# Four modulation buffers outside the Hyena block, and the last four modulation units spread over eight matrix units

## The chip, the cores and the metric

The kernel runs on one core of one Trainium2 chip. The metric is the device time of one execution in microseconds, lower is better. The engines that matter here are PE (TensorE, matrix products), DVE (VectorE), ACT (ScalarE) and SP (SyncE), which only issues DMA transfers.

## What is computed

A diffusion transformer of two layers on 256 latent tokens of width 2048, everything in float32. Layer 0 mixes tokens by attention (8 query heads, 2 key/value heads, with 256 context tokens) and by a gated short convolution, layer 1 by a Hyena long convolution through an FFT. Each layer ends with a squared-ReLU MLP of hidden width 8192. Every block is modulated by vectors that come from the condition c:

```python
def modulate(x, g, shift, scale):
    return rms_norm(x, g) * (1 + scale) + shift

def adaln(cond, w, b):
    return jnp.split(jax.nn.silu(cond) @ w + b, 6, axis=-1)
...
        sh1, sc1, g1, sh2, sc2, g2 = adaln(c[:, None, :], mod_w[l], mod_b[l])
...
            mix_l = jnp.concatenate([latent_attention(q_l, k_l, v_l, k_c, v_c),
                                     short_conv_mixer(pl[..., KV_HI:], ev_conv_w[e])], axis=-1)
            x = x + g1 * (mix_l @ ev_w_out[e])
...
            y = hyena_mixer(modulate(x, norm_mix_g[l], sh1, sc1), od_w_in[o], od_conv_w[o],
                            od_conv_b[o], hyena_filters(n, *fp), od_skip[o])
            x = x + g1 * (y @ od_w_out[o])
...
        x = x + g2 * ffn(modulate(x, norm_ffn_g[l], sh2, sc2), ffn_w1[l], ffn_w2[l])
```

So the weights are of two sorts: those of the large matrix products, with 256 columns of tokens, and `mod_w` (2 x 2048 x 12288), which meets a single vector.

## The kernel before

**Matrix units.** The large products are cut into 93 units. A unit is 2048 input rows by 512 output columns. SP brings its weights in four blocks of 1 MB into `w_raw[kg]`, kg = 0 to 3. ACT copies each block to the reduced float32r format (`w_hi`, two buffers, line 1184), DVE subtracts to get the remainder (`w_lo`, two buffers, line 737), and PE multiplies (line 478): per block 32 matmuls with `w_hi` and 16 with `w_lo`, 192 in a unit, into the four PSUM tiles `acc`. At the end of a unit DVE empties `acc` (line 777 by copy, line 820 into the residual `x`), and only then may PE begin the next (`psum_free`). The order of the units is: keys and values (unit 0), queries (1, 2), then attention, six units of the short convolution (3 to 8), four of the output product (9 to 12), the first MLP (13 to 44), Hyena (45 to 56) and its output (57 to 60), the second MLP (61 to 92).

**Modulation units.** Most of `mod_w` is taken by DVE instead of PE: a modulation unit (`mu`, 40 of them) is 512 columns in eight tiles of 128 x 1024 (512 KB), each loaded into `m_raw[i % 2]` and multiplied with the broadcast condition `wide`, with a sum along the row (line 745, called a tile below). After tile 7 two small operations add the parts and the bias (lines 749 and 751, the pair). `share(n, units, mods)` deals tiles to matrix units: units 0 to 11 take eight each, the first MLP five each, Hyena two or three each. The four modulation units of the last gate (mu 36 to 39) are taken eight tiles a unit in units 61 to 64.

**Who sets the order.** Each engine's program is written out by hand and waits on semaphores. DVE's part of unit u is `body`, where `part` is the unit's tiles in four shares, `fetched` empties `acc` and `post` is what follows (convolution, hidden activation, squares of `x`):

```python
                mod_tiles(part[0])
                lo(u, 2)
...
                mod_tiles(part[1])
                lo(u, 3)
                mod_tiles(part[2])
...
                    lo(u + 1, 0)
                mod_tiles(part[3])
                fetched()
...
                    lo(u + 1, 1)
```

SP issues all weight blocks and tiles from one queue, in program order (`unit`, lines 365 to 376, and `mod_tiles`, lines 354 to 361). It waits for `lo_done` ahead of a weight block (the block of the same kg of the unit before has been split) and for `m_steps` ahead of a tile (DVE has done the tile that had this buffer). With two buffers a tile waits for the one two places ahead of it. `convolution post` below means lines 1033, 1015 and 1022, which follow the second of each three convolution units.

## Time and profile before

| | us |
|---|---|
| median of 3 runs | 2762.68 (2758.9 to 2768.54) |
| the profiled execution's own time | 2763.58 |
| span of its trace | 2761.8 |
| PE busy | 2544.2 |
| DVE busy | 1820.8 |
| ACT busy | 955.9 |
| moved by DMA | 611.40 MB, mean 221 GB/s |

The span runs from the first to the last instruction; some 2 us of the execution's own time lie outside it. A busy share is a mean over stages. The stages here are: startup to 242 us, units 0 to 2 until 360, attention until 449, units 3 to 12 until 741, first MLP until 1518, Hyena and its output until 1961, second MLP to the end. In the waits, "A <- B" means that A stood idle until B had finished.

### The profile page before, as it was taken

What the parts mean: (1) busy time and instruction counts of PE and PEld (TensorE: products, weight loads), DVE (VectorE), ACT (ScalarE), POOL (GpSimd) and SP (SyncE); (2) the same over time, 40 slices, a digit from 0 to 9 for tenths busy, and PEclk for the clock granted to TensorE, in tenths of its full rate; (3) what the DMA queues carried; (4) which work ended last, traced back from release to release, by engine and by line L of the source; (5) the groups of instructions that cost most, each with busy time, mean ns of one, the idle gap of its engine ahead of it and who ended that gap; (6) DMA issues with size and microseconds to landing.
All of it is one profiled execution on the core that took longest, in us unless ns stands there. A gap on an engine that the chain in (4) does not pass through costs nothing.

```text
span 2761.8 us, 49389 instructions
## 1 busy us (share of the span) xinstructions
PE 2544.2 (92%) x19040; PEld 2355.4 (85%) x19040; DVE 1820.8 (66%) x2645; ACT 955.9 (35%) x958; POOL 0.2 (0%) x4
## 2 busy tenths in 40 slices
PE   6797978887899999999999899999879999999997
PEld 1224957887799999999999899999779999999997
DVE  1305665777787688787787778785776555555555
ACT  1314223222344333333343322233423333333333
POOL 0000000000000000000000000000000000000000
PEclk9798989998899999999999899999989999999998
DMA  7463824777578788788788556664586555555552
GB/s 269 140 197 131 279 87 149 273 271 280 199 273 293 261 292 300 274 297 298 266 296 297 185 197 216 234 222 157 167 283 215 181 182 182 182 182 181 182 182 101
DMA packets 266384, 611.40 MB, mean 221 GB/s; under 512 B 12245, under 2 KB 12373, under 8 KB 266014
## 3 DMA queue, kind: packets, MB, share of 16 engines
q1 hardware_dynamic: 260766, 598.93, 63.2%
q10 hardware_dynamic: 5504, 10.83, 1.1%
q8 instruction: 86, 1.41, 0.2%
q14 instruction: 28, 0.23, 0.0%
HBM read 603.43 MB, written 6.29 MB: 221 GB/s over the span
## 4 chain that ended last, share of the span: by engine, by line
PE 80%; DMA 8%; DVE 6%; issue 4%; ACT 2%; DVEq 0%; SPq 0%; ACTq 0%
PE acc L478 68%; DMA m_raw<-mod_rest 7%; PE acc L539 4%; PE aux L527 1%; PE aux L683 1%; PE aux L703 1%; DVE m_raw L745 1%; PE aux L475 1%; ACT w_hi L1184 1%; PE aux L516 1%; DVE summed L853 1%; PE acc L645 1%; DVE w_lo L737 1%; PE aux L519 0%; DVE x L820 0%
## 5 line engine op out<-in xcount | busy, mean ns | idle before, releaser
L737 DVE TENSOR_TENSOR w_lo<-w_raw,w_hi 128x2048 fp32r<-128x2048 f32 x372 | 851.1, 2289 | 459.9 <-ACT w_hi L1184 456.2
L1184 ACT ACTIVATE w_hi<-w_raw 128x2048 fp32r<-128x2048 f32 x372 | 712.1, 1915 | 1271.3 <-PE acc L478 1251.4
L478 PE MATMUL acc<-act_a,w_hi 128*128 128x256 f32 x6784 | 897.7, 290 | 70.4 <-DVE summed L777 30.8
L478 PEld LDWEIGHTS acc<-act_a,w_hi 128*128 128x128 f32 x6784 | 868.7, 198 | 76.9 <-issue 32.9
L478 PE MATMUL acc<-act_b,w_hi 128*128 128x256 f32 x5120 | 651.2, 286 | 28.6 <-DVE summed L777 14.8
L478 PEld LDWEIGHTS acc<-act_b,w_hi 128*128 128x128 f32 x5120 | 635.0, 195 | 31.2 <-DVE summed L777 15.4
L745 DVE SCALAR_TENSOR_TENSOR m_raw<-m_raw,wide 128x1024 f32<-128x1024 f32 x320 | 387.7, 1221 | 99.9 <-DMA m_raw<-mod_rest 99.2
L478 PE MATMUL acc<-act_a,w_lo 128*128 128x256 f32 x3392 | 448.8, 283 | 0.0
L478 PEld LDWEIGHTS acc<-act_a,w_lo 128*128 128x128 f32 x3392 | 426.7, 192 | 0.0
L478 PE MATMUL acc<-act_b,w_lo 128*128 128x256 f32 x2560 | 333.3, 283 | 0.0
L478 PEld LDWEIGHTS acc<-act_b,w_lo 128*128 128x128 f32 x2560 | 318.7, 192 | 0.0
L1184 ACT ACTIVATE act_b<-worked 128x256 f32 (+1 forms) x152 | 54.3, 420 | 203.3 <-DVE worked L798 122.5
L539 PE MATMUL acc<-w_raw,silu 128*2 128x512 f32 x256 | 115.1, 609 | 3.8 <-ACT late L1184 3.8
L890 DVE SCALAR_TENSOR_TENSOR summed<-worked,aux 128x512 f32<-128x512 f32 x16 | 10.3, 684 | 145.8 <-ACT worked L1184 145.8
L820 DVE SCALAR_TENSOR_TENSOR x<-acc,mv,x 128x256 f32 (+1 forms) x160 | 71.8, 481 | 49.6 <-PE acc L478 49.1
L539 PEld LDWEIGHTS acc<-w_raw,silu 128*2 128x2 f32 x256 | 21.5, 86 | 96.0 <-issue 91.4
L777 DVE COPY summed<-acc 128x256 f32<-128x256 f32 x192 | 75.4, 422 | 31.8 <-PE acc L478 27.2
L811 DVE TENSOR_TENSOR sq_sum<-sq_sum,worked 128x256 f32<-128x256 f32 x192 | 81.4, 424 | 21.2 <-ACT worked L1184 13.3
L1184 ACT ACTIVATE worked<-x 128x256 f32 (+1 forms) x176 | 62.1, 406 | 27.8 <-DVE x L820 23.9
L787 DVE TENSOR_TENSOR act_b<-worked,act_b 128x256 f32 (+1 forms) x152 | 54.4, 422 | 0.2 <-issue 0.2
L527 PE MATMUL aux<-scr,wide 128*128 128x512 f32 x64 | 38.1, 761 | 15.3 <-DVE scr L894 15.3
L527 PEld LDWEIGHTS aux<-scr,wide 128*128 128x128 f32 x64 | 15.5, 249 | 38.6 <-DVE scr L894 19.4
(129 smaller groups left out, 911.5 us busy)
## 6 DMA issues: line engine op xcount, KB each, us to landing
w_raw<-ffn_w SPq DMA_DIRECT2D x256, 1024.0 KB, 6.5
m_raw<-mod_rest SPq DMA_DIRECT2D x320, 512.0 KB, 5.2
w_raw<-od_w_in SPq DMA_DIRECT2D x48, 1024.0 KB, 7.0
w_raw<-ev_w_in SPq DMA_DIRECT2D x36, 1024.0 KB, 7.8
w_raw<-mod_first SPq DMA_DIRECT2D x32, 1024.0 KB, 5.2
w_raw<-ev_w_out SPq DMA_DIRECT2D x16, 1024.0 KB, 7.5
w_raw<-od_w_out SPq DMA_DIRECT2D x16, 1024.0 KB, 5.1
scr<-k_freq ACTq DMA_DIRECT2D x8, 512.0 KB, 5.8
```

The lines of the kernel that those rows point to most:

```text
L475: mm = pe.matmul(aux[ft][:, 0:n], w, act_b[:, k, a:a + n], start=start, stop=stop)
L478: mm = pe.matmul(acc[ft][:, 0:n], w, rhs[:, k, a:a + n], start=start, stop=stop)
L516: pe.matmul(aux[i][:, :], fh[0:FHID, i, tt * P:tt * P + P], m_raw[0:FHID, 0, i * 512:i * 512 + 512], start=True, stop=True)
L527: mm = pe.matmul(aux[r][:, :], fwd_first[:, tt, r * P:r * P + P], (f_sum if r < 2 else f_dif)[:, tt, :], start=(tt == 0), stop=(tt == 1))
L539: mm = pe.matmul(acc[tt][0:2, :], silu[:, 0, k:k + 17:16], w_raw[:, kg, kc * 512:kc * 512 + 512], start=(k == 0), stop=(k == 15))
L737: TT(w_lo[:, kg % 2, :], w_raw[:, kg, :], w_hi[:, kg % 2, :].bitcast(F32), ALU.subtract)\
L745: STT(out=raw, in0=raw, scalar=1.0, in1=wide[:, i % 2 * 1024:i % 2 * 1024 + 1024], op0=ALU.mult, op1=ALU.mult, accum_out=m_part[:, i:i + 1 ...
L777: dve.tensor_copy(dst, acc[ft][:, 0:T]).then_inc(psum_free, 1)
L787: TT(act_b[:, c, T:2 * T], worked[:, ft, :], act_b[:, c, 0:T].bitcast(F32), ALU.subtract)\
L811: TT(sq_sum[:, :], sq_sum[:, :], worked[:, slot, :], ALU.add).then_inc(sq_steps, 1)
L820: STT(out=xc, in0=acc[ft][:, 0:T], scalar=mv[:, ds(m * 4 + (gate + ft), 1)], in1=xc, op0=ALU.mult, op1=ALU.add).then_inc(psum_free, 1)
L1184: return act.activation(out_, in_, func, **kw)
```

## The change

- **Buffers.** Outside Hyena a tile goes to one of four buffers: the two halves of `m_raw` and two pieces of the scratch area `scr`. Up to unit 2 these are `scr[4096:5120]` and `scr[6144:7168]` (`EARLY`), afterwards `scr[2048:4096]` (`WIDE`), which attention uses for keys and values. In Hyena both sides of `scr` are in use, and the two buffers stay (`NARROW`). The wait is for the tile four places ahead (`i - 3`), in Hyena two (`i - 1`). There are four semaphores `m_landed`.
- **SP's order.** In unit u SP now issues, behind its four weight blocks in turn, tiles 4 and 5 of unit u-1, tiles 6 and 7 of unit u-1, tiles 0 and 1 of unit u, tiles 2 and 3 of unit u. This holds in Hyena too. Behind the fourth block of unit 3 SP waits for the end of attention (`o_full`), since tiles 2 and 3 go where keys and values were. The convolution units are written out instead of looped.
- **Second MLP.** The last four modulation units are dealt four tiles a unit to units 61 to 68, with the helper of the first MLP (`mlp_mods`, formerly `mlp0`).
- PE's and ACT's programs are the same.

```diff
+        def m_slots(early):
+
+            spare = (4096, 6144) if early else (2048, 3072)
+            return [m_raw[:, 0, :], m_raw[:, 1, :]] + [scr[:, a:a + 1024] for a in spare]
+
+        EARLY, WIDE = m_slots(True), m_slots(False)
+        NARROW = [m_raw[:, i % 2, :] for i in range(4)]
-        m_landed = [sem(f"m_landed{i}") for i in range(2)]
+        m_landed = [sem(f"m_landed{i}") for i in range(4)]
-            def mod_tiles(tiles):
+            def mod_tiles(tiles, slots):
 
                 for mu, i in tiles:
-                    if not (isinstance(mu, int) and mu == 0 and i < 2):
+                    if isinstance(mu, int) and mu == 0 and i < 4:
+                        if i == 2:
+                            sp.wait_ge(kf_full, 16)
+                            sp.wait_ge(row_turned, START)
+                    elif isinstance(mu, int) and mu == MU_F1 and i < 4:
+                        sp.wait_ge(m_steps, MU_F1 * 8)
+                    elif slots is NARROW:
                         sp.wait_ge(m_steps, mu * 8 + (i - 1))
-                    sp.dma_start(m_raw[:, i % 2, :], mod_rest[ds(mu * 512 + i // 2 * P, P), i % 2 * 1024:i % 2 * 1024 + 1024])\
-                        .then_inc(m_landed[i % 2], 16)
-
-            def unit(u, w, row, col, own=(), before=(), first=False):
+                    else:
+                        sp.wait_ge(m_steps, mu * 8 + (i - 3))
+                    sp.dma_start(slots[i % 4], mod_rest[ds(mu * 512 + i // 2 * P, P), i % 2 * 1024:i % 2 * 1024 + 1024])\
+                        .then_inc(m_landed[i % 4], 16)
+
+            def unit(u, w, row, col, own=(), before=(), first=False, slots=WIDE, old=None):
...
-                    mod_tiles(before[2 * kg + 2:2 * kg + 4] if kg < 3 else own[0:2])
+                    if kg < 2:
+                        mod_tiles(before[2 * kg + 4:2 * kg + 6], old or slots)
+                    else:
+                        mod_tiles(own[2 * kg - 4:2 * kg - 2], slots)
-            unit(U_KV, ev_w_in, 0, ATTN_W, mods(0), first=True)
-            unit(U_Q, ev_w_in, 0, 0, mods(1), mods(0))
-            unit(U_Q + 1, ev_w_in, 0, 512, mods(2), mods(1))
-            with sp.Fori(0, 2) as j:
-                for n, col in enumerate((2 * CONV_W, 0, CONV_W)):
-                    unit(j * 3 + (U_CONV + n), ev_w_in, 0, j * 512 + (KV_HI + col), mods(j * 3 + (3 + n)),
-                         mods(j * 3 + (2 + n)))
...
+            def conv_unit(j, n, old=None):
+                unit(j * 3 + (U_CONV + n), ev_w_in, 0, j * 512 + (KV_HI + (2 * CONV_W, 0, CONV_W)[n]),
+                     mods(j * 3 + (3 + n)), mods(j * 3 + (2 + n)), old=old)
+
+            for kg in range(4):
+                sp.wait_ge(lo_done, (U_CONV - 1) * 4 + (kg + 1))
+                sp.dma_start(w_raw[:, kg, :].rearrange("p (c n) -> p c n", c=4),
+                             ev_w_in[kg * 512:kg * 512 + 512, KV_HI + 2 * CONV_W:KV_HI + 2 * CONV_W + 512]
+                             .rearrange("(c p) n -> p c n", p=P)).then_inc(landed[kg], 16)
+                if kg < 2:
+                    mod_tiles(mods(2)[2 * kg + 4:2 * kg + 6], EARLY)
+                else:
+                    if kg == 3:
+                        sp.wait_ge(o_full, N_Q)
+                    mod_tiles(mods(3)[2 * kg - 4:2 * kg - 2], WIDE)
+            conv_unit(0, 1)
+            conv_unit(0, 2)
+            for n in range(3):
+                conv_unit(1, n)
             with sp.Fori(0, 3) as m:
                 unit(m + U_EVOUT, ev_w_out, 0, m * 512, mods(m + 9), mods(m + 8))
             unit(U_EVOUT + 3, ev_w_out, 0, 3 * 512, (), mods(11))
...
-            def mlp0(q, u, mu):
+            def mlp_mods(q, u, w_row, w2_row, mu, count, before):
+
 
                 for n in range(8):
-                    w, row, col = (ffn_w1, 0, q * 2048) if n < 4 else (ffn_w2, q * 2048, 0)
-                    if n:
-                        before = mods(mu, share(n - 1, 8, 5))
-                    else:
-                        before = () if isinstance(q, int) else mods(mu - 5, share(7, 8, 5))
-                    unit(u + n, w, row, col + n % 4 * 512, mods(mu, share(n, 8, 5)), before)
-
-            def mlp1(q, u, mod=None):
-
-                unit(u, ffn_w1, D_MODEL, q * 2048, mod(0) if mod else ())
-                with sp.Fori(1, 4) as m:
-                    unit(u + m, ffn_w1, D_MODEL, q * 2048 + m * 512, mod(m) if mod else (), mod(m - 1) if mod else ())
-                unit(u + 4, ffn_w2, q * 2048 + D_FF, 0, (), mod(3) if mod else ())
-                with sp.Fori(1, 4) as m:
-                    unit(u + m + 4, ffn_w2, q * 2048 + D_FF, m * 512)
-
-            mlp0(0, U_F0, MU_F0)
+                    w, row, col = (ffn_w1, w_row, q * 2048) if n < 4 else (ffn_w2, q * 2048 + w2_row, 0)
+                    unit(u + n, w, row, col + n % 4 * 512, mods(mu, share(n, 8, count)),
+                         mods(mu, share(n - 1, 8, count)) if n else before)
+
+            mlp_mods(0, U_F0, 0, 0, MU_F0, 5, ())
...
+            def hyena(j, before, old=NARROW):
                 for n, col in enumerate((1, 2, 0)):
                     unit(j * 3 + (U_D - 3 + n), od_w_in, 0, j * 512 + (col * D_MODEL - 512),
                          mods(j + (MU_D - 1), share(n, 3, 1)),
-                         mods(j + (MU_D - 1), share(n - 1, 3, 1)) if n else before)
-
-            hyena(1, mods(MU_D - 5, share(7, 8, 5)))
+                         mods(j + (MU_D - 1), share(n - 1, 3, 1)) if n else before, slots=NARROW, old=None if n else old)
...
+            hyena(1, mods(MU_D - 5, share(7, 8, 5)), WIDE)
+            sp.wait_ge(b_made, 96)
+            mlp_mods(0, U_F1, D_MODEL, D_FF, MU_F1, 4, ())
             with sp.Fori(1, 4) as q:
-                mlp1(q, q * 8 + U_F1)
+                u = q * 8 + U_F1
+                with sp.Fori(0, 4) as m:
+                    unit(u + m, ffn_w1, D_MODEL, q * 2048 + m * 512)
+                with sp.Fori(0, 4) as m:
+                    unit(u + m + 4, ffn_w2, q * 2048 + D_FF, m * 512)
...
-            def mod_tiles(tiles):
+            def mod_tiles(tiles, slots):
 
                 for mu, i in tiles:
-                    dve.wait_ge(m_landed[i % 2], mu * 64 + 16 * (i // 2 + 1))
-                    raw = m_raw[:, i % 2, :]
+                    dve.wait_ge(m_landed[i % 4], mu * 32 + 16 * (i // 4 + 1))
+                    raw = slots[i % 4]
                     STT(out=raw, in0=raw, scalar=1.0, in1=wide[:, i % 2 * 1024:i % 2 * 1024 + 1024], op0=ALU.mult,
                         op1=ALU.mult, accum_out=m_part[:, i:i + 1]).then_inc(m_steps, 1)
...
-            body(U_KV, keys_values, mod=0)
+            body(U_KV, keys_values, mod=0, slots=EARLY)
             with own.loop(2, 0) as m:
-                body(m + U_Q, lambda: queries(m), mod=m + 1)
...
-                    body(u + m, lambda: sums(u + m), lambda: hidden(u + m, m, q * 16 + f0 + m * 4), mod(m) if mod else None)
+                    body(u + m, lambda: sums(u + m), lambda: hidden(u + m, m, q * 16 + f0 + m * 4))
                 clear_squares(step)
-                if mod:
-                    dve.wait_ge(mv_ready, MU_F1 + 4)
```

Two places of SP's program on which terms of the prediction rest. The first is between the last query unit and the second convolution unit. SP's program before, from the last weight block of unit 2 (`L373`) on; the loop over the convolution units begins with the branch, and its rows that are not DMA are register work and waits:

```order
L373 DMA w_raw<-ev_w_in 128x4x512 [waits lo_done]
L360 DMA m_raw<-mod_rest 128x1024 [waits m_steps] x2
L401 UNCONDITIONAL_BRANCH
L401 ISA
L373 ISA [waits lo_done]
L373 DMA w_raw<-ev_w_in 128x4x512
L359 ISA
L360 ISA [waits m_steps]
L360 DMA m_raw<-mod_rest 128x1024
```

SP's program of the change, from the third weight block of unit 3 on:

```order
L427 DMA w_raw<-ev_w_in 128x4x512 [waits lo_done]
L376 DMA m_raw<-mod_rest 128x1024 [waits m_steps] x2
L427 DMA w_raw<-ev_w_in 128x4x512 [waits lo_done]
L376 DMA scr<-mod_rest 128x1024 [waits m_steps,o_full]
L376 DMA scr<-mod_rest 128x1024 [waits m_steps]
L389 DMA w_raw<-ev_w_in 128x4x512 [waits lo_done]
L376 DMA m_raw<-mod_rest 128x1024 [waits m_steps] x2
```

Two tiles still follow each weight block, now by turns in `m_raw` and `scr`, and tiles 2 and 3 of unit 3 have the wait for `o_full` ahead of them, and behind them stands the first weight block of unit 4. The second place is the first three Hyena units, 45 to 47. SP's program before, from the third block of unit 45 on:

```order
L373 DMA w_raw<-od_w_in 128x4x512 [waits lo_done] x2
L360 DMA m_raw<-mod_rest 128x1024 [waits m_steps] x2
L373 DMA w_raw<-od_w_in 128x4x512 [waits lo_done] x4
L360 DMA m_raw<-mod_rest 128x1024 [waits m_steps] x2
L373 DMA w_raw<-od_w_in 128x4x512 [waits lo_done]
L360 DMA m_raw<-mod_rest 128x1024 [waits m_steps]
L373 DMA w_raw<-od_w_in 128x4x512 [waits lo_done] x3
```

and SP's program of the change, from the second block of unit 45 on:

```order
L389 DMA w_raw<-od_w_in 128x4x512 [waits lo_done] x2
L376 DMA m_raw<-mod_rest 128x1024 [waits m_steps] x2
L389 DMA w_raw<-od_w_in 128x4x512 [waits lo_done] x4
L376 DMA m_raw<-mod_rest 128x1024 [waits m_steps] x2
L389 DMA w_raw<-od_w_in 128x4x512 [waits lo_done]
L376 DMA m_raw<-mod_rest 128x1024 [waits m_steps]
L389 DMA w_raw<-od_w_in 128x4x512 [waits lo_done] x3
```

The rows look alike, but they stand for other blocks. Before, the four loads in one row are the blocks of unit 46, the tile pair behind them its tiles 2 and 3, and the single load is the first block of unit 47, behind which comes tile 4. Now the four are the last block of unit 45 and the first three of unit 46, the single load is the last block of unit 46, and tile 4 stands behind it, ahead of the first block of unit 47.

## Rows read from the trace of the kernel before

**Rows 1.** Page: busy time of each engine, share of the span, instructions.
```profile
PE 2544.2 (92%) x19040; PEld 2355.4 (85%) x19040; DVE 1820.8 (66%) x2645; ACT 955.9 (35%) x958; POOL 0.2 (0%) x4
```

**Rows 2.** Windows: start:end length, busy us (x count) per engine, clock, DMA share, GB/s.
```profile
303.65:359.67 56.02, 47.99 (x387) 47.59 (x385) 42.49 (x58) 15.33 (x8) 0.00 (x0) 0.96 0.81 279
448.84:627.82 178.98, 148.83 (x1153) 147.61 (x1153) 131.83 (x193) 47.41 (x28) 0.00 (x0) 0.91 0.81 278
627.82:716.22 88.40, 75.01 (x576) 74.40 (x576) 67.72 (x96) 27.61 (x24) 0.00 (x0) 0.90 0.80 284
1976.97:2097.16 120.19, 98.84 (x760) 98.03 (x758) 92.05 (x141) 38.52 (x35) 0.00 (x0) 0.90 0.79 268
766.30:789.30 23.00, 23.00 (x194) 23.00 (x193) 20.27 (x28) 9.06 (x9) 0.00 (x0) 1.00 0.89 311
473.95:501.04 27.09, 24.78 (x193) 24.58 (x193) 20.34 (x27) 7.66 (x4) 0.00 (x0) 0.94 0.92 320
593.97:627.82 33.85, 24.80 (x193) 24.60 (x193) 25.82 (x43) 7.67 (x4) 0.00 (x0) 0.86 0.72 247
1420.00:1430.00 10.00, 10.00 (x85) 10.00 (x85) 9.99 (x19) 4.11 (x6) 0.00 (x0) 1.00 1.03 391
```

**Rows 3.** Waits 448 to 742: who waited for whom, us in total, times, longest.
```profile
DVE m_raw L745 <- DMA m_raw<-mod_rest: 52.6, 46, 3.0
...
PE acc L478 <- DVE summed L777: 23.2, 4, 9.0
...
PE acc L478 <- DVE x L820: 13.4, 3, 5.8
```

**Rows 4.** Timeline 464 to 513: start, us, engine, line, op, [idle before].
```profile
464.49 1.92 ACT L1184 ACTIVATE w_hi<-w_raw 128x2048 fp32r<-128x2048 f32 x1 [3.85 <-PE acc L478]
...
466.53 2.29 DVE L737 TENSOR_TENSOR w_lo<-w_raw,w_hi 128x2048 fp32r<-128x2048 f32 x1
...
498.87 1.22 DVE L745 SCALAR_TENSOR_TENSOR m_raw<-m_raw,wide 128x1024 f32<-128x1024 f32 x1 [1.11 <-DMA m_raw<-mod_rest]
...
500.56 1.41 DVE L777 COPY summed<-acc 128x256 f32<-128x256 f32 x4
...
501.04 5.59 PE L478 MATMUL acc<-act_a,w_hi 128*128 128x256 f32 x32 [2.31 <-DVE summed L777]
...
501.89 2.28 DVE L737 TENSOR_TENSOR w_lo<-w_raw,w_hi 128x2048 fp32r<-128x2048 f32 x1
504.09 1.43 DVE L1033 TENSOR_TENSOR summed<-summed,scr 128x256 f32<-128x256 f32 x4
...
509.92 1.22 DVE L745 SCALAR_TENSOR_TENSOR m_raw<-m_raw,wide 128x1024 f32<-128x1024 f32 x1
...
512.21 2.29 DVE L737 TENSOR_TENSOR w_lo<-w_raw,w_hi 128x2048 fp32r<-128x2048 f32 x1
```

**Rows 5.** Timeline 345 to 362, the end of the second query unit.
```profile
358.19 1.42 DVE L777 COPY scr<-acc 128x256 f32 x4
...
359.67 1.97 PE L593 MATMUL acc<-tab,scr 128*128 128x128 f32 x8 [3.69 <-DVE scr L777]
```

**Rows 6.** Chain that ended last, piece of the last 28 units.
```profile
2097.16 646.43 PE acc L478 x5364
```

**Rows 7.** Timeline of PE 1998 to 2125, first units of the second MLP.
```profile
2007.24 5.60 PE L478 MATMUL acc<-act_a,w_hi 128*128 128x256 f32 x32 [7.07 <-DVE summed L777]
...
2103.57 2.08 PE L478 MATMUL acc<-act_b,w_lo 128*128 128x256 f32 x16
```

**Rows 8.** Waits of PE 752 to 1530, the first MLP.
```profile
PE acc L478 <- issue: 12.6, 3, 4.6
...
PE acc L478 <- DVE summed L777: 1.0, 1, 1.0
```

**Rows 9.** Page, DMA issues: count, KB each, median us to landing.
```profile
m_raw<-mod_rest SPq DMA_DIRECT2D x320, 512.0 KB, 5.2
w_raw<-od_w_in SPq DMA_DIRECT2D x48, 1024.0 KB, 7.0
```

More of the change, by code:

```diff
@@ L397, in _ @@
             sp.wait_ge(h_full, 8)
-            unit(U_KV, ev_w_in, 0, ATTN_W, mods(0), first=True)
-            unit(U_Q, ev_w_in, 0, 0, mods(1), mods(0))
-            unit(U_Q + 1, ev_w_in, 0, 512, mods(2), mods(1))
-            with sp.Fori(0, 2) as j:
-                for n, col in enumerate((2 * CONV_W, 0, CONV_W)):
-                    unit(j * 3 + (U_CONV + n), ev_w_in, 0, j * 512 + (KV_HI + col), mods(j * 3 + (3 + n)),
-                         mods(j * 3 + (2 + n)))
+            unit(U_KV, ev_w_in, 0, ATTN_W, mods(0), first=True, slots=EARLY)
+            unit(U_Q, ev_w_in, 0, 0, mods(1), mods(0), slots=EARLY)
+            unit(U_Q + 1, ev_w_in, 0, 512, mods(2), mods(1), slots=EARLY)
+            def conv_unit(j, n, old=None):
[16 more added lines that the diff above has]
+                conv_unit(1, n)
             with sp.Fori(0, 3) as m:
@@ L752, in mod_tiles, with body @@
                            vec[:, ds(mu * 4 + (VEC["mod_b"][0] + 32), 4)], ALU.add).then_inc(mv_ready, 1)
-            def body(u, fetched, post=None, mod=None, tiles=EIGHT, mid=None, last=False):
+            def body(u, fetched, post=None, mod=None, tiles=EIGHT, mid=None, last=False, slots=WIDE):
                 tiles = [] if mod is None else [(mod + m, i) for m, i in tiles]
                 part = [tiles[len(tiles) * i // 4:len(tiles) * (i + 1) // 4] for i in range(4)]
-                mod_tiles(part[0])
+                mod_tiles(part[0], slots)
                 lo(u, 2)
@@ L762, in body @@
                     mid()
-                mod_tiles(part[1])
+                mod_tiles(part[1], slots)
                 lo(u, 3)
-                mod_tiles(part[2])
+                mod_tiles(part[2], slots)
                 if not last:
                     lo(u + 1, 0)
-                mod_tiles(part[3])
+                mod_tiles(part[3], slots)
                 fetched()
@@ L1066, in mlp0, with mlp @@
                         clear_squares(step)
-                    v, tiles = u + n, share(n, 8, 5)
+                    v, tiles = u + n, share(n, 8, count)
+                    gate = 80 + 96 * layer
                     if n >= 4:
-                        body(v, lambda: residual(v, n - 4, 80, 9 + n),
+                        body(v, lambda: residual(v, n - 4, gate, first_gate + n - 3),
                              lambda: x_squares(xu + (n - 4), step + (n * 4 - 15)), mu, tiles)
                     else:
-                        body(v, lambda: sums(v), lambda: hidden(v, n, q * 16 + (16 + n * 4)), mu, tiles)
-            def mlp(q, u, layer, f0, xu, step, mod=None, final=False):
+                        body(v, lambda: sums(v), lambda: hidden(v, n, q * 16 + f0 + n * 4), mu, tiles)
+            def mlp(q, u, layer, f0, xu, step, final=False):
                 with own.loop(4, 0) as m:
-                    body(u + m, lambda: sums(u + m), lambda: hidden(u + m, m, q * 16 + f0 + m * 4), mod(m) if mod else None)
+                    body(u + m, lambda: sums(u + m), lambda: hidden(u + m, m, q * 16 + f0 + m * 4))
                 clear_squares(step)
-                if mod:
-                    dve.wait_ge(mv_ready, MU_F1 + 4)
                 gate = 80 + 96 * layer
@@ L1151, in hyena @@
                     body(j * 3 + (U_D + n), lambda: sums(j * 3 + (U_D + n)), lambda: post(j),
-                         j + MU_D, share(n, 3, 1),
+                         j + MU_D, share(n, 3, 1), slots=NARROW,
                          mid=None if n or first else (lambda: convolved(j - 1)))
```

13 lines of the change are left out of this document (6 added, 7 removed).

## The prediction

> **What bounds the kernel now.** I read the busy shares first. PE is busy for 2544.2 us, 92% [rows 1], so the kernel is bound by PE plus the places where PE stands. Next I asked what one matrix unit takes when nothing is in its way. The last piece of the chain of waits runs over the last 28 units (65 to 92) in 646.43 us [rows 6]; less 2.6 us for a slow start (below) that is 23.0 us a unit. The stretch 766.30 to 789.30, in the first MLP with five tiles a unit, shows the same: PE busy for all 23.00 us [rows 2]. So 23.0 us is the floor.
>
> Then the windows of the stages with eight tiles a unit [rows 2]. Units 1 and 2 take 56.0 us (floor 46.0), the six convolution units 179.0 us (138.0), units 9 to 11 88.4 us (69.0), and units 61 to 64 120.2 us (92.0). The granted clock there is 0.90 to 0.96 instead of 1.00. What ends PE's waits is DVE emptying `acc`: 23.2 us in four waits and 13.4 us in three [rows 3]. What delays DVE is its own wait for tiles, 52.6 us in 46 waits [rows 3]. The chain reads: a tile lands late, DVE reaches the evacuation late, PE starts the next unit late. Each late start costs twice. At 501.04 PE had been idle for 2.31 us, and its first 32 matmuls took 5.59 us [rows 4] instead of the 4.0 us of others; the granted clock over that unit is 0.94 [rows 2], so for a moment it was the lower of the two levels, 1.2 instead of 2.4 GHz. I take 1.6 us for this slow group behind a wait of about 2 us or more, and up to 2.6 us behind longer ones.
>
> **The change part by part.** It adds no arithmetic: 320 tiles, the same pairs, the same PE program. It gives a tile four places of lead instead of two. At the floor a place is 23.0 / 8 = 2.9 us; four of them less the 1.15 us of the tile itself leave 10.3 us from the issue to the need, against 4.6 us with two. The median landing time is 5.2 us [rows 9]: longer than 4.6, shorter than 10.3. So I remove DVE's waits for tiles and ask what is late next.
>
> DVE's own work in a unit with eight tiles [rows 4]: a tile 1.15 us (509.92 to 512.21 is two), so 9.2; the pair 0.54 (498.87 to 500.56, less a tile), so 0.6; four `w_lo` at 2.2 (501.89 to 504.09), so 8.8; the evacuation 1.33 (500.56 to 501.89). Sum 19.9 us. The convolution post adds 5.8 (504.09 to 509.92) in every third unit, the others less: about 3 for the gate and 2 for the squares, estimates from the four-instruction groups of 1.4 us.
>
> *An ordinary unit.* Let PE start at S. ACT's copy for the next unit's first block comes 15.6 us later (464.49, where S is 448.9), DVE's `w_lo` at S + 17.6 (466.53). Add 2.2, two tiles 2.3 and the pair 0.6: the evacuation starts at S + 22.7, and PE follows 0.48 behind it (500.56 to 501.04), at S + 23.2. That is 0.2 over the floor, with too short a wait for a slow group (estimate).
>
> *Units 1 and 2.* Unit 2 starts at 326.7 instead of 331.2, without its slow group, and its evacuation begins at 326.7 + 22.8 = 349.5. The transposes of attention follow 1.48 us behind such a start (358.19 to 359.67 [rows 5]), at 351.0 instead of 359.67: **8.6 us** gained. Attention itself keeps its length. At its end tiles 2 and 3 of unit 3 now wait for `o_full`, and the first block of unit 4 is queued behind them. Tiles 2 and 3 are needed some 9 us after it, the block some 15: with 5.2 and 7 us to land, that costs nothing.
>
> *Convolution and output, units 3 to 11.* Unit 3: 23.2. Unit 4: 23.2. Behind unit 4 DVE has the post, and its cycle from one evacuation to the next is 19.9 + 5.8 = 25.7 us, which puts unit 6 at 49.0 us behind the start of unit 4 instead of 46.2. Unit 5 therefore lasts 26.0 with 2.8 us of waiting at its end, and unit 6 has the slow group, 24.8. Units 7, 8 and 9 repeat 4, 5 and 6; units 10 and 11 take 23.2. Sum: 23.2 + 23.2 + 26.0 + 24.8 + 23.2 + 26.0 + 24.8 + 23.2 + 23.2 = 217.6 us, against 267.4 (448.84 to 716.22 [rows 2]): 49.8 gained, and 1.6 for the slow group of unit 12: **51.4 us**.
>
> *First MLP.* It has one wait for DVE of 1.0 us [rows 8], 1.2 with its edges, behind a late tile: **1.2 us**. The three waits marked issue, 12.6 us together [rows 8], fall where PE's own loop turns back; PE's program is the same, and I leave them.
>
> *Second MLP.* PE stood for 7.1 us ahead of unit 62, which began at 2007.24 [rows 7]; units 62 to 64 took 89.9 us (2007.24 to 2097.16 [rows 6, 7]) for 69.1; unit 65 had a slow group of 6.4 instead of 3.8 (2097.16 to 2103.57). Excess 7.1 + 20.8 + 2.6 = 30.5. With four tiles in eight units, fewer than the five under which the first MLP runs at its floor [rows 2], all of it goes: **30.5 us**.
>
> *Hyena.* Still two buffers, but the single tile now stands ahead of the first weight block of the next unit. That block is issued about 10 us into a unit and needed at 15.6 to 17; it takes 7.0 us to land [rows 9]. PE itself needs the result only at 23.0, so I cost it at nothing. Bounds: a gain of nothing, a loss of 2 us in each of eight units, 16 us.
>
> *The transfers.* Eleven units (1 to 11) move 92.3 MB (8.39 MB each). By the sums above they last 47.4 + 217.6 = 265.0 us, which asks for 348 GB/s, and 363 GB/s in those near the floor. The trace before bounds this from both sides: 320 GB/s at a DMA share of 0.92 in the best unit with eight tiles, 391 GB/s over the best 10 us [rows 2]. 320 at 0.92 means about 348 at a full share, 311 at 0.89 about 349. I take 349, the nearest kind of row, which makes 24.0 us for each of the five units that are not slowed by the post (1, 2, 9 to 11): 0.8 to 1.0 each, **5 us** lost. At 391 it is 0, at 320 it is 23.
>
> A page of the Trainium skill speaks against part of this: "DMA: Bandwidth & Descriptors", section Specifications, gives about 358 GB/s as the limit of HBM for one core, by which, as an estimate, a unit would take 23.4 us and the loss would be 2 us instead of 5; that changes no chance, since it stays inside my forecast's spread. The 391 GB/s of [rows 2] are above it, if only for 10 us.
>
> Sum: 8.6 + 51.4 + 1.2 + 30.5 - 5 = 86.7 us off 2763.6, the profiled execution's own time: 2676.9. The median of the runs is 0.9 below that execution, so 2676.
>
> **Rivals.**
> - *DMA bound.* At the best unit's 320 GB/s the eleven units take 288.4 instead of 270 us: 2695. For it: 320 was reached while tiles were late, so much was queued. Against it: the share there was 0.92, not 1. Chance 0.15.
> - *Late by a little.* If a tile or block still comes 1 us late in each of eleven units, every start has its wait and its slow group: 11 x 2.6 = 29 us, less the 5 already counted: 2700. For it: landing is 5.2 us in the median, not at most. Chance 0.08.
> - *Better.* The transfers cost nothing and the post's 10 us are partly hidden, or the issue waits shrink: 2663. Chance 0.09.
> - *It does not do what it says.* One SP queue in program order: tiles are held behind weight blocks that wait, and the lead stays at two in the stages with eight tiles. Then only 30.5 and 1.2 us remain: 2731, taken from 2762.7. Against it: a block's wait (`lo_done` of the unit before) is nearly always fulfilled when its turn comes. Chance 0.04.
> - *Slower.* The mix of tiles and blocks, more of them in flight, moves at a lower rate. At the 247 GB/s of unit 8 (593.97 to 627.82), the lowest window [rows 2], the eleven units take 374 us instead of 323.4, a loss of 50 against 32 gained elsewhere: 2781. It decides below 92.3 MB / 355 us = 260 GB/s. Unit 8 shows 247 GB/s, but at a DMA share of 0.72, so it was short of requests and not of rate, and the windows of whole stages lie at 278 and more [rows 2]. Chance 0.02.
> - *No change* from causes that cancel: 0.02.
>
> **The numbers.** My forecast has 0.60. Predicted 2676. The forecast's own spread is 2668 to 2686; down to the better case and up over both DMA cases, 2660 to 2704, leaves out some 0.1. A measurement of this kernel tells 0.3%, 8 us, from no change. Faster 0.96, same 0.02, slower 0.02.
>
> **What would show it.** Right: DVE's waits for tiles between the end of startup and the second MLP nearly gone; unit lengths of 23 to 24 us, with 26 for units 5 and 8; units 61 to 68 at 23.0; DMA near 350 GB/s in units 1, 2 and 9 to 11; attention and Hyena as long as before; three issue waits left. Wrong: `w_hi` on ACT waiting for `w_raw` from DMA, in Hyena above all, or unit lengths of 26 us with the DMA share near 1.

## The result and the profile after

The changed kernel takes 2667.14 us in the median of 4 runs (2661.42 to 2669.68), beside 2760.79 before (2757.38 to 2768.54): ratio 0.9655, 95% interval 0.9632 to 0.9677. The forecast was 2676, with a range from 2660 to 2704. The two profiled executions have spans of 2761.8 and 2667.9 us, 93.9 apart, and the stages are compared on these.

The page of the changed kernel: busy time, granted clock and rate in 40 slices, the chain that ended last, the groups of the tiles (they answer to [rows 1]) and the DMA issues (as [rows 9]).

```profile
PE 2517.2 (94%) x19040; PEld 2327.9 (87%) x19040; DVE 1812.4 (68%) x2645; ACT 955.7 (36%) x958; POOL 0.2 (0%) x4
...
PEclk9788989999899999999998999999899999999998
...
GB/s 278 144 170 188 251 97 159 340 335 334 220 291 295 292 294 299 281 297 291 288 298 215 208 195 189 228 231 154 189 274 273 202 175 186 185 177 189 177 185 94
...
PE 86%; DVE 7%; DMA 2%; issue 2%; ACT 2%; DVEq 0%; SPq 0%; ACTq 0%
...
L774 DVE SCALAR_TENSOR_TENSOR m_raw<-m_raw,wide 128x1024 f32<-128x1024 f32 x176 | 211.9, 1217 | 0.4
L774 DVE SCALAR_TENSOR_TENSOR scr<-scr,wide 128x1024 f32<-128x1024 f32 x144 | 173.2, 1219 | 0.0
...
m_raw<-mod_rest SPq DMA_DIRECT2D x176, 512.0 KB, 5.6
scr<-mod_rest SPq DMA_DIRECT2D x144, 512.0 KB, 6.4
w_raw<-od_w_in SPq DMA_DIRECT2D x48, 1024.0 KB, 8.5
```

DVE stood 0.4 us ahead of all 320 tiles together; before, 52.6 us between 448 and 742 alone [rows 3]. A tile takes longer to land than before (5.6 and 6.4 us, not 5.2 [rows 9]) and is still in time. A block of `od_w_in` takes 8.5 instead of 7.0 [rows 9], which matters below.

Windows of the changed kernel (start:end length, busy us of each engine, clock, DMA share, GB/s): unit 2, units 4 to 8, one of them, unit 11, and units 62 to 65 (by the marks of the table below), to be held against [rows 2]:

```profile
309.00:332.00 23.00, 22.89 (x191) 22.68 (x190) 20.59 (x29) 7.26 (x5) 0.00 (x0) 1.00 0.91 337
443.40:563.50 120.10, 117.71 (x962) 116.93 (x962) 106.37 (x154) 39.72 (x24) 0.00 (x0) 0.99 0.96 358
467.00:490.00 23.00, 23.00 (x192) 22.87 (x192) 19.81 (x28) 7.45 (x5) 0.00 (x0) 1.00 1.01 373
614.00:637.60 23.60, 23.35 (x194) 23.15 (x194) 21.85 (x32) 9.29 (x9) 0.00 (x0) 1.00 0.96 345
1918.30:2009.90 91.60, 91.60 (x766) 91.60 (x765) 72.77 (x101) 36.41 (x33) 0.00 (x0) 1.00 0.78 264
```

PE is busy for 118 of 120 us in units 4 to 8; before, it stood for 30 of the 179 us of units 3 to 8 [rows 2]. The DMA engines carry 373 GB/s over a whole unit.

What each stage gave, measured from ACT's copy of the third block of one unit to that of the next (so "unit 6" ends when PE has been in unit 6 for 4 us, or for 5.6 us where it began slowly, and holds PE's wait ahead of it); the forecast has the price of the transfers dealt out as it was counted:

| stage | forecast | measured |
|---|---|---|
| startup and unit 0 | 0 | -0.8 |
| units 1 to 3, attention between them | 8.6 - 2.0 | 10.4 |
| units 4 to 12 | 51.4 - 3.0 | 51.1 |
| units 13 to 20 | 1.2 | 1.3 |
| the first MLP behind them, all of it in units 21, 29 and 37 | 0 | 12.9 |
| Hyena and its output, units 45 to 60 | 0 | -10.5 |
| second MLP | 30.5 | 30.2 |
| sum | 86.7 | 94.6 |

(0.7 us of it is lost behind the last unit, which leaves the 93.9 of the spans.) The mark of unit 0 lies anywhere from 270.7 to 273.9 us in the twelve traces of this case, whatever the edit, so 3 us between two whole times say nothing of an edit. The two large rows forecast as zero nearly cancel. The experiments are about these two, and about which part of the change does what.

**Where Hyena lost.** Waits of the changed kernel, 1470 to 1910:

```profile
ACT w_hi L1213 <- DMA w_raw<-od_w_in: 51.9, 11, 8.0
...
PE acc L507 <- DVE summed L806: 5.9, 4, 2.0
```

Neither wait exists before in this stage. Its timeline in PE's unit 52, where the first block of unit 53 is fetched (start, us, engine, line, op, idle before):

```profile
1664.27 0.08 DVE L774 DVE_READ_ACCUMULATOR m_raw<-m_raw,wide 128x1 f32 x1
1664.53 0.33 SPq L376 DMA_DIRECT2D m_raw<-mod_rest  x1
...
1665.16 1.67 SPq L389 DMA_DIRECT2D w_raw<-od_w_in  x3
...
1673.08 1.92 ACT L1213 ACTIVATE w_hi<-w_raw 128x2048 fp32r<-128x2048 f32 x1 [7.64 <-DMA w_raw<-od_w_in]
...
1677.33 1.22 DVE L774 SCALAR_TENSOR_TENSOR m_raw<-m_raw,wide 128x1024 f32<-128x1024 f32 x1
...
1678.47 1.42 DVE L806 COPY summed<-acc 128x256 f32<-128x256 f32 x4
...
1678.95 2.31 PE L507 MATMUL acc<-act_a,w_hi 128*128 128x256 f32 x14 [2.03 <-DVE summed L806]
```

Unit 52 began on PE at 1653.72. With two buffers the tile's request waits for the tile two places ahead, done at 1664.27. Three weight blocks stand behind it in SP's queue and are requested together, at 1665.16 and after. The first is there at 1673.08, 19.4 us into the unit; ACT could have copied it at 15.6. DVE is then late at the evacuation, PE stands for 2.03 us, and a slow group follows: from mark to mark (unit 53 of the table's measure) this took 26.8 us instead of 23.0.

**Where the first MLP gained.** Units 21, 29 and 37 hold the places where PE's own loop over the quarters turns back. They took 30.0, 29.7 and 30.0 us before and take 25.1, 26.7 and 25.0 now; the `issue` waits of [rows 8] are gone and these stand there (waits of PE in the changed kernel, 700 to 1470):

```profile
PE acc L507 <- DVE x L849: 5.5, 3, 2.0
```

Before: the first turn, timeline of PE and DMA queues (share of 16 engines) from 943 to 945.

```profile
940.39 2.08 PE L478 MATMUL acc<-act_b,w_lo 128*128 128x256 f32 x16
946.61 1.65 PE L478 MATMUL acc<-act_a,w_hi 128*128 128x256 f32 x6 [4.14 <-issue]
...
q1 hardware_dynamic: 301, 0.76, 102.1%
q8 instruction: 1, 0.02, 3.2%
```

After: the same turn, DMA queues from 879 to 881.

```profile
878.35 2.08 PE L507 MATMUL acc<-act_b,w_lo 128*128 128x256 f32 x16
882.26 1.94 PE L507 MATMUL acc<-act_a,w_hi 128*128 128x256 f32 x14 [1.83 <-DVE x L849]
...
q1 hardware_dynamic: 122, 0.42, 73.7%
q8 instruction: 1, 0.02, 3.9%
```

### The profile page after: what moved, and what is told of

The parts are those of the page before. It is cut to its first block, busy times and chain, and to the rows that moved or that the text cites. A ratio compares the mean times of both kernels' runs of the same rounds, so it can differ in the third digit from the quotient of the medians.

```text
span 2667.9 us, 48783 instructions
## 1 busy us (share of the span) xinstructions
PE 2517.2 (94%) x19040; PEld 2327.9 (87%) x19040; DVE 1812.4 (68%) x2645; ACT 955.7 (36%) x958; POOL 0.2 (0%) x4
## 4 chain that ended last, share of the span: by engine, by line
PE 86%; DVE 7%; DMA 2%; issue 2%; ACT 2%; DVEq 0%; SPq 0%; ACTq 0%
PE acc L507 74%; PE acc L568 4%; PE aux L556 1%; DMA w_raw<-od_w_in 1%; DVE w_lo L766 1%; PE aux L712 1%; PE aux L504 1%; ACT w_hi L1213 1%; PE aux L732 1%; PE aux L545 1%; DMA scr<-k_freq 1%; DVE m_raw L774 1%; PE acc L674 1%; DVE x L849 0%; PE aux L548 0%
## 5 line engine op out<-in xcount | busy, mean ns | idle before, releaser
L507 PE MATMUL acc<-act_a,w_hi 128*128 128x256 f32 x6784 | 879.1, 286 | 29.6 <-DVE act_a L887 14.5
L507 PEld LDWEIGHTS acc<-act_a,w_hi 128*128 128x128 f32 x6784 | 850.0, 194 | 36.1 <-issue 19.7
L507 PE MATMUL acc<-act_b,w_hi 128*128 128x256 f32 x5120 | 643.1, 284 | 3.5 <-DVE summed L806 2.4
L507 PEld LDWEIGHTS acc<-act_b,w_hi 128*128 128x128 f32 x5120 | 627.2, 192 | 5.7 <-DVE x L849 2.6
L774 DVE SCALAR_TENSOR_TENSOR m_raw<-m_raw,wide 128x1024 f32<-128x1024 f32 x176 | 211.9, 1217 | 0.4
L774 DVE SCALAR_TENSOR_TENSOR scr<-scr,wide 128x1024 f32<-128x1024 f32 x144 | 173.2, 1219 | 0.0
L849 DVE SCALAR_TENSOR_TENSOR x<-acc,mv,x 128x256 f32<-128x256 f32 (+1 forms) x160 | 71.5, 481 | 43.9 <-PE acc L507 43.9
L840 DVE TENSOR_TENSOR sq_sum<-sq_sum,worked 128x256 f32<-128x256 f32 x192 | 81.4, 424 | 22.5 <-ACT worked L1213 13.9
L816 DVE TENSOR_TENSOR act_b<-worked,act_b 128x256 fp32r<-128x256 f32 (+1 forms) x152 | 54.2, 420 | 0.2 <-issue 0.2
```

Of the source, the lines that this page charges most:

```text
L507: mm = pe.matmul(acc[ft][:, 0:n], w, rhs[:, k, a:a + n], start=start, stop=stop)
L774: STT(out=raw, in0=raw, scalar=1.0, in1=wide[:, i % 2 * 1024:i % 2 * 1024 + 1024], op0=ALU.mult, op1=ALU.mult, accum_out=m_part[:, i:i + 1 ...
L816: TT(act_b[:, c, T:2 * T], worked[:, ft, :], act_b[:, c, 0:T].bitcast(F32), ALU.subtract)\
L840: TT(sq_sum[:, :], sq_sum[:, :], worked[:, slot, :], ALU.add).then_inc(sq_steps, 1)
L849: STT(out=xc, in0=acc[ft][:, 0:T], scalar=mv[:, ds(m * 4 + (gate + ft), 1)], in1=xc, op0=ALU.mult, op1=ALU.add).then_inc(psum_free, 1)
```

## The experiments

Each is one edit to the changed kernel unless said otherwise. The edits are shown in part, `...` marks what is left out, and ratios are to the kernel before on the same chip, which had a median of 2761.15 (experiments 1 to 4), 2764.47 (5 to 8) and 2761.98 (9 and 10).

### 1. Hyena with SP's old order

```diff
+                    if slots is NARROW and old is not WIDE:
+                        mod_tiles(before[2 * kg + 2:2 * kg + 4] if kg < 3 else own[0:2], slots)
...
```

> The changed kernel, but in Hyena SP issues in the order of the kernel before: the single tile behind the first weight block of the next unit, the tile pair behind the last block of its own unit. Theory A (a weight block queued behind a tile that waits, then three blocks at once, comes too late for ACT): the 11 us that units 46 to 57 lost against before come back, 2656, and ACT's waits for od_w_in from DMA (51.9 us in the changed kernel) fall under 10. Rival B (Hyena lost by another phase of the k_freq loads or of DVE, not by the order of SP): 2667 as the changed kernel.

Measured: 2655.93 us (2653.07 to 2659.26), ratio 0.9626 (0.9591 to 0.9661). Units 47, 50, 53 and 56 are back at 23.0 us, and ACT waits for no block of `od_w_in` any more. The loss in Hyena comes from the order of SP's queue, not from the bus: the same bytes move with the same two buffers.

### 2. First MLP with two buffers and the old order

```diff
+                    elif order == "old":
+                        mod_tiles(before[2 * kg + 2:2 * kg + 4] if kg < 3 else own[0:2], slots)
...
-            mlp_mods(0, U_F0, 0, 0, MU_F0, 5, ())
+            mlp_mods(0, U_F0, 0, 0, MU_F0, 5, (), slots=NARROW, order="old")
...
```

> The changed kernel, but the first MLP has two buffers and SP's order of before; everything else of the change stays. It tells where the 12.9 us at the three turns of PE's loop came from (units 21, 29 and 37 took 30.0, 29.7, 30.0 us from second to third ACT copy before, 25.1, 26.7, 25.0 in the changed kernel). Theory A (PE fetches its instructions over the same DMA engines, and the fetch at a turn stands behind whatever SP had just issued; with the old order more is queued there): the three turns take 30 us again, the issue waits of PE are back at 4 us each, the late tile of unit 17 is back, 2681. Rival B (the turns have nothing to do with the tiles' order; an effect of alignment elsewhere): 2667 to 2669.

Measured: 2679.81 us (2678.02 to 2681.77), ratio 0.9709 (0.9674 to 0.9743). The edit also changes where SP issues the last tiles of the first MLP, in the first Hyena unit; Hyena as a whole loses 8.9 us here. The turn units are at 30.7, 29.8 and 30.0. The waits of PE there:

```profile
PE acc L511 <- issue: 14.0, 3, 5.0
```

So the length of PE's loop turns depends on how SP issues. Buffers or order? The next one tells.

### 3. Four buffers, but the old order everywhere

```diff
-                    if kg < 2:
-                        mod_tiles(before[2 * kg + 4:2 * kg + 6], old or slots)
-                    else:
-                        mod_tiles(own[2 * kg - 4:2 * kg - 2], slots)
...
+                    mod_tiles(before[2 * kg + 2:2 * kg + 4] if kg < 3 else own[0:2], old if kg < 3 else slots)
...
```

The wait for the end of attention moves with the tiles, behind the first block of unit 4.

> Four buffers outside Hyena and the spread of the last four modulation units, but everywhere SP's order of the kernel before. Theory A (what counts is four places of lead; SP's order only costs in Hyena): units 3 to 12 as in the changed kernel within 5 us, Hyena as before, 2655 to 2662 by where the loop turns of the first MLP land. Rival B (the new order is needed, since with the old one the second pair of tiles stands behind the first weight block of the next unit): tile waits on DVE return in units 1 to 12, over 20 us, 2690 or more.

Measured: 2669.9 us (2667.95 to 2672.04), ratio 0.9677 (0.9643 to 0.9711). Units 3 to 12 and the second MLP are as in the changed kernel (units 6 and 9 27.6 and 26.6, unit 10 22.8), Hyena is as before, but the turn units take 29.1, 29.4 and 29.7 with the wait back:

```profile
PE acc L508 <- issue: 13.1, 3, 4.6
```

The expectation was missed because it took the shorter turns for a gift of the four buffers. They come from the new order. So the buffers (with the spread) give the gains in units 1 to 12 and the second MLP, and the new order gives some 11 us at the turns and takes as much in Hyena: the two kernels' intervals overlap.

### 4. The new order with two buffers everywhere

```diff
-        EARLY, WIDE = m_slots(True), m_slots(False)
-        NARROW = [m_raw[:, i % 2, :] for i in range(4)]
+        EARLY = WIDE = NARROW = [m_raw[:, i % 2, :] for i in range(4)]
...
```

> SP's new order and the spread, but two buffers everywhere. Theory A (lead is what counts; at two places it is 4.6 us against 5.2 to land): the waits of DVE for tiles return in units 1 to 12 in full, and weight blocks are in addition held behind tiles that wait; 60 us of the gain are lost and some more, 2725 to 2760. Rival B (the order alone brings most of it): under 2690.

Measured: 2828.08 us (2820.28 to 2829.22), ratio 1.0239 (1.02 to 1.0278): slower than before by some 67 us, and outside what was expected. The spread is in this kernel too and is worth 30 us by itself (experiment 5), so by the two ratios the new order costs some 98 us where there are two buffers. The whole trace's waits:

```profile
ACT w_hi L1208 <- DMA w_raw<-ffn_w: 367.4, 73, 8.4
...
DVE m_raw L769 <- DMA m_raw<-mod_rest: 62.6, 51, 3.0
```

and the timeline in the first MLP, where five tiles a unit ran at the floor before:

```profile
817.16 4.02 SPq L371 DMA_DIRECT2D m_raw<-mod_rest  x2
...
821.22 0.43 SPq L384 DMA_DIRECT2D w_raw<-ffn_w  x1
...
827.57 1.91 ACT L1208 ACTIVATE w_hi<-w_raw 128x2048 fp32r<-128x2048 f32 x1 [6.55 <-DMA w_raw<-ffn_w]
```

SP stands at the second of two tiles until a buffer is free, and the weight block behind it goes out late. The first MLP alone loses 75 us, with nearly every unit at 24 to 28. This is what happened in Hyena, at two or three tiles a unit, made large. The new order asks for tiles earlier, and with no free buffer to take them that only holds up the blocks.

### 5. The kernel before, with only the last modulation units spread

```diff
-            mlp1(0, U_F1, lambda m: mods(m + MU_F1))
+            mlp0(0, U_F1, MU_F1, D_MODEL, D_FF, 4)
...
```

> The kernel before (two buffers, old order) with the spread of the last four modulation units over units 61 to 68 alone. Theory A (four tiles a unit leave two buffers enough lead, as five do in the first MLP): all 30.5 us of the second MLP are gained and nothing else changes, 2730. Rival B (it needs four buffers as well): DVE's tile waits stay in part, 2740 or more.

Measured: 2730.43 us (2727.51 to 2733.54), ratio 0.9885 (0.9866 to 0.9904). Units 62 to 65 take 22.5 to 23.0 us. This is also the time that the rival "it does not do what it says" named.

### 6. The changed kernel without the spread

```diff
+    if (units, mods) == (8, 4):
+        return [(n, i) for i in range(8)] if n < 4 else []
```

> The changed kernel without the spread: eight tiles in each of units 61 to 64, with four buffers. Theory A (DVE needs 19.9 us and 3 us of post in such a unit, so four buffers alone nearly suffice): 23.2 to 23.8 us a unit, 2668 to 2671. Rival B (eight tiles a unit need the spread, since transfers or DVE are too slow there): units of 25 us or more, 2676 or more.

Measured: 2664.53 us (2663.79 to 2667.3), ratio 0.9646 (0.9629 to 0.9663), no slower than with it. Window over units 62 to 65, eight tiles each:

```profile
1912.40:2004.20 91.80, 91.80 (x767) 91.80 (x766) 89.53 (x137) 36.40 (x32) 0.00 (x0) 1.00 0.94 344
```

PE has no gap and DVE is busy for 89.5 of 91.8 us. So either part alone gives the 30 us of the second MLP, and with four buffers the spread is idle.

### 7. Evacuation ahead of the last two tiles in units 5 and 8

On top of experiment 1.

```diff
+                if soon:
+                    fetched()
                 mod_tiles(part[3], slots)
-                fetched()
+                if not soon:
+                    fetched()
...
```

> Hyena in the old order of SP (as in the run before, 2656) and in units 5 and 8 DVE empties the accumulators ahead of the last two tiles of the unit instead of behind them. Theory A (units 5 and 8 last 27.2 us from copy to copy because DVE, with the convolution post, reaches the evacuation 3 us late): PE starts units 6 and 9 without a wait and without its slow group, 4 us each, 2648. Rival B (DVE's work in the three units is the bound, so what is saved at unit 6 is lost at its end): 2655.

Measured: 2654.21 us (2653.19 to 2657.31), ratio 0.9609 (0.9592 to 0.9627). From the mark of unit 3 to that of unit 12 its trace takes 214.3 us, that of experiment 1 takes 217.7. PE does start units 6 and 9 without a wait, but it then stands ahead of units 7 and 10. PE in both, first experiment 1, then this one:

```profile
509.55 5.58 PE L511 MATMUL acc<-act_a,w_hi 128*128 128x256 f32 x32 [2.38 <-DVE summed L810]
583.16 5.42 PE L511 MATMUL acc<-act_b,w_hi 128*128 128x256 f32 x32 [2.39 <-DVE summed L810]
...
531.52 4.10 PE L511 MATMUL acc<-act_a,w_hi 128*128 128x256 f32 x32 [2.26 <-DVE scr L813]
603.62 4.09 PE L511 MATMUL acc<-act_b,w_hi 128*128 128x256 f32 x32 [2.55 <-DVE x L856]
```

The waits are as long as in experiment 1, 4.8 us for the two: what is saved ahead of unit 6 is lost ahead of unit 7, as rival B says. Of the 3.4 us, 2.8 are the first groups behind the waits, 5.58 and 5.42 us there, 4.10 and 4.09 here. The granted clock over the two groups here is 1.00. In the whole time, 2654.21, this can't be told from experiment 1 or from rival B's 2655: one of its turn units took 26.7 instead of 24.8 us, again by a slow first group.

### 8. PE's loop over the quarters of the first MLP written out

```diff
-            with pe.Fori(0, 4) as q:
+            for q in range(4):
```

> The changed kernel with PE's loop over the four quarters of the first MLP written out, so that PE has no jump back at units 21, 29 and 37. Theory A (the rest of the waits there, 25.1, 26.7 and 25.0 us for 23.0, is the fetch of instructions behind a jump): these units take 23.0, 7.8 us gained, 2659. Rival B (the waits come from DVE or from the transfers of weights at that place): 2667. It could also cost, if PE then waits for instructions all along.

Measured: 2657.25 us (2651.88 to 2658.75), ratio 0.961 (0.9591 to 0.9629). The turn units take 23.5, 23.4 and 23.4. So what remained of the turns in the changed kernel was the loop's own.

### 9. More data in front of the instructions

```diff
+                    if spare and kg == 3:
+                        for a in (4096, 6144 - 1024):
+                            sp.dma_start(scr[:, a:a + 1024], mod_rest[0:P, 0:1024]).then_inc(spare_landed, 16)
+                        sp.dma_start(scr[:, 6144:7168], mod_rest[0:P, 0:1024]).then_inc(spare_landed, 16)
+                        sp.dma_start(scr[:, 0:1024], mod_rest[0:P, 0:1024]).then_inc(spare_landed, 16)
...
+                    if n == 3 and not isinstance(q, int):
+                        sp.wait_ge(spare_landed, q * 64)
```

> The changed kernel, with four more transfers of 512 KB each (modulation weights, read into a buffer that nobody uses) requested behind the last weight block of the first unit of quarters 1 to 3 of the first MLP; the computation is unchanged. Theory A (at a loop turn TensorE's instructions are fetched over the same DMA engines and stand behind whatever data is queued there): each of the three turn units 21, 29 and 37 grows from about 25 to 29 or 30 us, issue waits of TensorE come back in the list of waits, the time is about 2680. Theory B (the length of a turn has nothing to do with queued data): the turn units stay at 25 to 27 us, no issue waits, 2665 to 2671.

Measured: 2677.36 us (2673.65 to 2679.42), ratio 0.9696 (0.9675 to 0.9717). The turn units are at 29.4, 28.9 and 29.3 us, the others as they were. The waits of PE in the first MLP, PE at the first turn, and the DMA queues from 881 to 882:

```profile
PE acc L515 <- issue: 13.4, 3, 4.7
...
876.95 2.08 PE L515 MATMUL acc<-act_b,w_lo 128*128 128x256 f32 x16
883.75 3.50 PE L515 MATMUL acc<-act_a,w_hi 128*128 128x256 f32 x15 [4.72 <-issue]
...
q1 hardware_dynamic: 108, 0.38, 102.2%
q8 instruction: 1, 0.02, 6.1%
```

PE finished at 879.03. The instruction packet starts at 881.0 and takes 0.97 us (6.1% of 16 engines for 1 us), so PE starts 1.8 us behind its end, as in the two traces above. PE's program and the tiles are those of the changed kernel; only queued data was added, and 10.8 of the 12.9 us came back.

The same is seen at every turn. Ten of the twelve traces keep PE's loop (all but experiments 8 and 10), which makes 30 turns. By the DMA records PE starts 1.75 to 1.88 us behind the end of such a packet in all 30. In the 18 turns of the kernel before and of experiments 2, 3, 4, 5 and 9 the packet begins 0.8 to 2.2 us after PE has run dry, and the data queue's share in the 2 us ahead of it was 0.98 or more. In the 12 of the changed kernel and of experiments 1, 6 and 7 it begins 0.8 to 1.2 us before PE is done, at a share of 0.50 to 0.96.

### 10. Experiments 1, 7 and 8 together

> Three edits to the changed kernel at once: the Hyena block goes back to the old order of its requests with two modulation buffers, units 5 and 8 put their evacuation before their last two tiles, and TensorE's loop over the quarters of the first MLP is written out. Theory A (the three act at different places and so add up): 2655.9 from the Hyena edit alone, less 7 to 10 us for the loop turns, less 2 to 4 us for the evacuations, about 2646. Theory B (the gains overlap, because work that comes earlier only meets the next late transfer): 2652 to 2656, no better than the Hyena edit with the evacuations.

Measured: 2647.81 us (2647.33 to 2649.67), ratio 0.9589 (0.9571 to 0.9606), the fastest of all. The page and the window over units 4 to 8:

```profile
span 2647.4 us, 48550 instructions
...
PE 91%; DVE 5%; issue 2%; ACT 1%; DMA 1%; DVEq 0%; ACTq 0%; SPq 0%
```

```profile
443.40:563.50 120.10, 117.82 (x977) 117.20 (x977) 108.06 (x159) 41.50 (x25) 0.00 (x0) 1.00 0.97 362
```

It is 19 us below the changed kernel: by the trace 10.8 in Hyena (units 45 to 60) and 6.6 in the turn units (76.8 down to 70.2). Of the 20.5 us between the two spans that leaves 3.1, and the trace is ahead by as much at unit 12, behind the two evacuations that were moved.

## Why the prediction was right

**What bounds the kernel** held: late tiles, late evacuation, late PE. With the lateness gone DVE's waits for tiles are gone and ordinary units take 23.2 to 23.5 us.

**Units 3 to 11** held nearly to the term: 51.4 less 3 forecast, 51.1 measured. The working of the post (of `convolution post`) is visible as it was put. Timeline of the changed kernel at the end of unit 5:

```profile
510.96 1.41 DVE L806 COPY summed<-acc 128x256 f32<-128x256 f32 x4
...
511.44 5.58 PE L507 MATMUL acc<-act_a,w_hi 128*128 128x256 f32 x32 [2.39 <-DVE summed L806]
```

PE waits 2.39 us (2.8 forecast; the 26.0 of the sum should have been 25.7 by its own cycle of DVE) and then has the slow group of 5.58 instead of 4.0. Unit 6 by the table's marks is 27.2 us; 2.8 and 1.6 over 23.2 would be 27.6.

**The slow group** was priced rightly at 1.6 us, but in part by a wrong row: the clock of 0.94 is that of the unit ahead of 501.04, which had a slow group of its own at 473.95. The group at 501.04 itself shows 0.69:

```profile
501.04:503.50 2.46, 2.46 (x15) 2.46 (x16) 2.46 (x4) 0.00 (x0) 0.00 (x0) 0.69 0.89 288
```

That it comes behind "a wait of about 2 us or more" came true in units 6 and 9 and is no rule (experiment 7, and the last section).

**Units 1 and 2**: the products of attention begin at 352.05 us, against 351.0 forecast and 359.67 before, so 7.6 of the 8.6 came; the 2 us taken off for transfers did not. "Attention itself keeps its length" did not hold: up to unit 3 it takes 87.3 us instead of 89.2. The 1.9 us lie in its first products, 11.5 instead of 13.6 us up to PE's first long wait, at a granted clock of 0.67 instead of 0.50, behind a wait of 1.08 instead of 3.69 us.

**The transfers** were mis-sized: 5 us forecast. The step that failed is the one from "320 GB/s at a share of 0.92" to "348 at a full share". A share did not stand for the same rate in the two kernels: the changed one shows 337 at 0.91, 358 at 0.96 and 373 at 1.01, which is some 370 for a full share, where the rows before gave 349. Units 10 to 12 still took 0.3 us each over the 23.2 of the forecast, so about 1 of the 5 us may be real. The rival "DMA bound" is out: its 320 GB/s are passed in every window above with eight tiles a unit. The Trainium skill's figure of 358 GB/s for a core ("DMA: Bandwidth & Descriptors", Specifications) is passed too, over a whole unit; the section Measured of the same page gives 425 for a single core in transfers of 16 MB, and the highest window shown here, 404 over 2.6 us, stays below it.

**First MLP, issue waits**: the step "PE's program is the same, and I leave them" failed. The program was the same, but the time in which its instructions arrive was not: 12.9 us gained. The forecast looked for what PE waits for among engines and data only. Experiments 2, 3 and 9 bring these waits back and experiment 8 removes what is left of them, all with the same matrix products. Of the 12.9 us, 7.1 are shorter waits (12.6 and 5.5 us for the three) and 5.7 are the first groups behind them: 6.69, 6.57 and 6.20 us before, 4.10, 5.59 and 4.09 now, which is also why unit 29 takes 26.7 and not 25.

**Hyena** was costed at nothing, within bounds from 0 to 16; 10.5 were lost, and 7.2 to 8.9 in the traces of experiments 2, 6, 8 and 9, which keep the new order there. The place and the mechanism were named (the tile ahead of the first block of the next unit, 7.0 us to land, needed at 15.6), and so was the sign of a miss, ACT waiting for `w_raw`. Two things were sized wrong. The block goes out at 11.4 us into the unit, not 10, since SP stands at the tile until its buffer is free. And 7.0 us was the median of blocks requested one by one, while here three go out within 1.7 us behind a tile: from 1660 to 1700 they took 6.3 to 11.8 us, 8.9 in the median. The nearest row for a bunched request was not the median of single ones.

**Second MLP** held (30.5 and 30.2), but the reason was only half of it: four buffers alone do the same (experiment 6).

**The sum** came within 9 us because two misses of 12.9 and -10.5 cancel, which is luck; the rest of the difference is the transfers and the attention stage. 2667.14 is just below the forecast's own spread (2668 to 2686), inside its range, and nearer to the rival "better", 2663, than to 2676. That rival had the right conditions in part (transfers free, issue waits shrunk). The rival "slower" names bytes that move at a lower rate; the rate rose. "Late by a little" came true only in Hyena.

## What to carry to other kernels

More lead for a load is worth something only with a free buffer to take it: an earlier place without the buffer stops everything behind it (experiment 4, 67 us over the kernel before), while the buffers and the spread with the old places gave as much as the whole change (experiment 3). Before moving requests in a shared queue, write down at each one what it waits for, which urgent load stands behind it, and how many go out at once when the wait ends. And a wait marked `issue` where an engine's loop turns back belongs to the DMA traffic as much as to the program; write the loop out, or keep the queue short there.
